# A hybrid decoder step on one core: earlier memory statistics, half-waits in the first quarters, and a head's output scaled on ScalarE

## What is computed

```python
hp = rms_norm(yp, g_norm[l])
qd, kd, vd, gd, qw, kw, vw, gw, qm, gm = split_projection(hp, w_in[l])
od = diff_attn_prompt(qd, kd, vd, lam, slopes_diff)      # 4 heads, softmax(q1 k1) - lam * softmax(q2 k2)
ow = dilated_prompt(qw, kw, vw, slopes_dil)
mk, mv = memory_kv(mem_prompt, g_mem_norm[l], w_mem_kv[l])   # rms_norm(mem) @ w_mem_kv
om = memory_attn(qm, mk, mv)
...
od = rms_norm(od, g_sub) * (1.0 - lam_init)              # per head, over its 256 values
cat = concatenate([od * silu(gd), ow * silu(gw), om * silu(gm)])
yp = yp + cat @ w_out
```

## Time and profile before

| | |
|---|---|
| median of 3 runs | 1027.82 us (1025.97 to 1028.28) |
| the profiled execution's own time | 1026.25 us |
| its span in the trace | 1024.5 us |
| granted TensorE clock | 0.997 |
| busy: PE, DVE, ACT, POOL | 1000.5, 723.7, 441.5, 54.7 us |

### The profile page before, as it was taken

The page is one execution under the profiler, slowest core; times in us unless marked ns, Lnnn a source line. Parts: engine busy times, 40 slices in busy tenths (PEclk is TensorE's granted clock), DMA queues, the critical chain, the costliest instruction groups (busy, mean ns, idle before and its releaser), DMA issues.

```text
span 1024.5 us, 24055 instructions
## 1 busy us (share of the span) xinstructions
PE 1000.5 (98%) x8103; PEld 980.4 (96%) x8103; DVE 723.7 (71%) x2687; ACT 441.5 (43%) x1169; POOL 54.7 (5%) x122
## 2 busy tenths in 40 slices
PE   7999999999999999999999999999999999999995
PEld 6899999999999999999999999999999999999995
DVE  5783267777788867778777676577774786588874
ACT  5763222222333333444342553335565365545552
POOL 0200000000000000000000000000000100000002
PEclk9999999999999999999999999999999999999998
DMA  9863288987978877777866686999662425234424
GB/s 300 250 195 107 64 266 265 293 271 226 266 220 254 259 231 235 219 224 207 245 200 192 186 249 181 231 280 284 193 191 72 140 74 153 94 104 145 124 84 167
DMA packets 254521, 203.33 MB, mean 198 GB/s; under 512 B 12480, under 2 KB 207670, under 8 KB 253750
## 3 DMA queue, kind: packets, MB, share of 16 engines
q1 hardware_dynamic: 253934, 200.67, 65.7%
q10 hardware_dynamic: 464, 1.12, 0.3%
HBM read 189.98 MB, written 11.76 MB: 197 GB/s over the span
## 4 chain that ended last, share of the span: by engine, by line
PE 91%; DVE 2%; ACT 2%; issue 2%; SPq 1%; DMA 1%; POOL 0%; DVEq 0%; POOLq 0%; ACTq 0%
PE z L1097 71%; PE z L1123 8%; PE o_ps L1193 2%; PE s_ps L1156 2%; PE t_ps L1143 2%; PE t_ps L1183 1%; PE s_ps L1161 1%; DMA w_raw<-in_w_mem_kv_dram 1%; PE o_ps L1198 1%; PE o_ps L1202 1%; PE s_ps L1168 1%; PE o_ps L1242 1%; ACT w_hi L1351 1%; PE s_ps L1028 1%; SPq L828 1%
## 5 line engine op out<-in xcount | busy, mean ns | idle before, releaser
L1097 PE MATMUL z<-act_hi,w_hi 128*128 128x260 f32 (+1 forms) x2048 | 440.9, 291 | 2.4 <-DVE act_lo L1629 2.3
L1097 PE MATMUL z<-act_hi,w_lo 128*128 128x260 f32 (+1 forms) x2048 | 422.4, 283 | 0.0
L1097 PE MATMUL z<-act_lo,w_hi 128*128 128x260 f32 (+1 forms) x2048 | 421.6, 282 | 0.0
L1097 PEld LDWEIGHTS z<-act_hi,w_hi 128*128 128x128 f32 x2048 | 321.5, 189 | 7.9 <-issue 4.0
L1097 PEld LDWEIGHTS z<-act_lo,w_hi 128*128 128x128 f32 x2048 | 319.9, 188 | 0.0
L1097 PEld LDWEIGHTS z<-act_hi,w_lo 128*128 128x128 f32 x2048 | 319.5, 188 | 0.0
L1676 DVE TENSOR_TENSOR w_lo<-w_raw,w_hi 128x512 fp32r<-128x512 f32 x302 | 206.8, 687 | 132.5 <-ACT w_hi L1351 131.8
L1351 ACT ACTIVATE w_hi<-w_raw 128x512 fp32r<-128x512 f32 x302 | 186.4, 626 | 200.4 <-PE z L1097 173.2
L1865 DVE CUSTOM_DVE_ANT_0 pages<-pages,q_bc 128x128 f32<-128x128 f32 x640 | 144.2, 285 | 21.2 <-DMA pages<-in_cache_k_win_dram 13.5
L1894 DVE SCALAR_TENSOR_TENSOR v_acc<-pages,dec_a,v_acc 128x256 f32<-128x256 f32 x224 | 94.3, 478 | 1.7 <-DMA pages<-in_cache_v_diff_dram 1.5
L1473 ACT ACTIVATE probs<-probs,st_n 128x128 f32<-128x128 f32 (+3 forms) x48 | 26.8, 558 | 79.9 <-DVE st_n L1804 79.6
(11 more groups left out here) (236 smaller groups left out, 1121.8 us busy)
## 6 DMA issues: line engine op xcount, KB each, us to landing
w_raw<-in_w_in_dram SPq DMA_DIRECT2D x224, 256.0 KB, 4.5
pages<-in_cache_k_diff_dram SPq DMA_DIRECT2D x128, 256.0 KB, 4.7
pages<-in_cache_v_diff_dram SPq DMA_DIRECT2D x128, 256.0 KB, 3.6
w_raw<-in_w_out_dram SPq DMA_DIRECT2D x64, 256.0 KB, 2.8
w_raw<-in_w_mem_kv_dram SPq DMA_DIRECT2D x32, 256.0 KB, 6.1
cat<-in_x_prompt_dram SPq DMA_DIRECT2D x8, 1024.0 KB, 6.0
q_bc<-q_rows_dram SPq DMA_DIRECT2D x32, 256.0 KB, 6.7
pages<-in_cache_mem_k_dram SPq DMA_DIRECT2D x16, 256.0 KB, 6.4
```

Source lines behind the costliest of these rows:

```text
L1097: last = nc.tensor.matmul(zb[:, bank, 0:b - a], lhs[:, w], rhs[:, kt, a:b], start=(kt == 0 and m == 0), stop=(kt == KT - 1 and m == 2))
```

## The change

There are four kinds of edits. In the tables of `plan()`, the memory squares go from slot 5 to 2 and the factor from slot 9 to 7; the first two key tiles are evacuated at slots 8 and 9 instead of 10 and 11, and turned at slots 10 and 11 instead of 11 and 13. `qrows` 2 goes from slot 177 to 178, and part 1 of the memory group's softmax from slot 196 to 195. In `quarter`, the first input tile and the first memory tile wait for the split activations before each pair of blocks instead of before all four. In a differential head, ACT waits for POOL's factor right behind the squares and scales `o_ps` into `o_nat` itself; DVE's scaling is dropped.

```diff
-    put(5, "mem", "squares")
-    put(9, "mem", "rstd")
+    put(2, "mem", "squares")
+    put(7, "mem", "rstd")
...
-            put(s + (6, 3)[n] if n < 2 else s, "evac", n, 0.65 if kind in ("gd", "gw") else 1.3 if kind == "gm" else 0.0)
+            put(s + (4, 1)[n] if n < 2 else s, "evac", n, 0.65 if kind in ("gd", "gw") else 1.3 if kind == "gm" else 0.0)
         if kind in ("mk", "mv", "kd", "kw", "vd", "vw"):
-            put(s + (7, 5)[n] if n < 2 else s + (2 if n < FIRST_IN else 1), "nat", n)
+            put(s + (6, 3)[n] if n < 2 else s + (2 if n < FIRST_IN else 1), "nat", n)
...
-    put(DONE[AT["qm", 3, 0]] + 1, "qrows", 2)
+    put(DONE[AT["qm", 3, 0]] + 2, "qrows", 2)
...
-                put(s0 + SOFT_AT[k], "soft", (what, k), 0.6)
+                put(s0 + SOFT_AT[k] - (what == MEMORY and k == 1), "soft", (what, k), 0.6)
...
                 if n == FIRST_IN:
-                    pe.wait_ge(s_plo, prep_base(2) + 2 * r + 2)
                     pe.wait_ge(s_xsl, 1)
-                if n == 0:
-                    pe.wait_ge(s_plo, 2 * r + 2)
...
                 for j in range(4):
                     kt = 4 * r + j
                     w = slice(j * P, (j + 1) * P)
+                    if n in (0, FIRST_IN) and j % 2 == 0:
+                        pe.wait_ge(s_plo, prep_base(0 if n == 0 else 2) + kt // 2 + 1)
...
                         nc.scalar.activation(o_nat[:, :], o_ps[:, 0:2 * P], ACT.Square,
                                              accum_out=st_q[:, 0, 0:1]).then_inc(s_osq, 1)
+                        act.wait_ge(s_orstd, what + 1)
+                        nc.scalar.activation(o_nat[:, :], o_ps[:, 0:2 * P], ACT.Copy, scale=st_q[:, 1, 0:1]).then_inc(s_ofree, 1)
...
                 if kind == "diff":
-                    dve.wait_ge(s_orstd, t + 1)
-                    nc.vector.tensor_scalar(o_nat[:, :], o_ps[:, 0:2 * P], st_q[:, 1, 0:1], None, ALU.mult).then_inc(s_ofree, 1)
+                    return
```

## The result

The changed kernel takes 1028.19 us (median of 22 runs, 1026.5 to 1030.95), the kernel before 1026.74 us (median of 22, 1025.82 to 1028.28). The ratio is 1.0015 with a 95% interval of 1.0009 to 1.0021: some 1.5 us slower, less than the 0.2% that the prediction called no change. Predicted was 1028.5 us. The profiled execution took 1027.94 us with a span of 1026.2 us. One execution each of three later kernels (*rows_early*, *soft_half*, *scale_only*) took 1407 to 5631 us; the ratios leave these three out, the medians still count them.

A forecast was written before the change was run, and what follows sets the result against it. PE was taken as the bound, busy 1000.5 of 1024.5 us, so only its waits counted. Key tiles +1.2, query rows +0.3 and memory softmax -0.8 gave +0.7 us on 1027.82, hence 1028.5 us, range 1025.0 to 1031.0.

The forecast's parts named there:

- likeliest case: Whole kernel: gains and losses balance as summed, or no move reaches PE's end; 1026.8 to 1029.8 us, chance 0.60.
- query rows: Slot 178: an old 0.8 us wait goes, a new 1.1 us wait comes near 567 us; net 0.3 us lost.
- key tiles: Start: ACT's second key copy waits for the first's store, ahead of split and squares; quarter 16 starts 1.2 us later.
- Half-waits, squares, factor: Start: half-waits gain at most 2.3 us, PE stands 2.3 us for diagonals; 0.6 us loss, hidden by the key tiles.
- Rival (a): Key and row stores land by themselves, key store in 1.9 us, both new waits vanish; -2.7 us, 1025.1, chance 0.18.
- Rival (b): Slot 178: the row store stays as slow as before, 3.8 us; +2.9 us, 1030.7, chance 0.18.
- The scaling: Sixteen differential heads: ACT gains about 0.8 us of wait and 0.3 us of scaling each, hidden; no cost taken.
- Rival (c): Differential heads: ACT, blocked about 1.1 us sixteen times, delays PE 0.3 us per step; +4.8 us, 1033.3, chance 0.04.
- Memory softmax: Part 1 one slot earlier no longer stands behind the bank's copy it waited for; 0.8 us gained.

The follow-up runs named there:

- rows_early: The changed kernel with the query rows' copy (`qrows` 2) back at slot 177; 1026.84 us, ratio 0.9997 to the kernel before.
- soft_half: The kernel before with only squares at slot 2, the half-waits and the softmax part one slot earlier; 1026.13 us, ratio 0.9987.
- scale_only: The kernel before with the scaling of the differential heads' output on ACT as its only edit; 1027.31 us, ratio 1.0001.
- factor_late: The changed kernel with the factor back at slot 9 and the first two key tiles' evacuation and turning where they were; 1027.37 us, ratio 1.0006.
- diag_first: rows_early with DVE building the factor's diagonals ahead of the split of quarter 10; 1026.25 us, ratio 0.9997 to the kernel before.
- head_only: The kernel before with only the edits of the start (squares, factor, first key tiles, half-waits); 1027.86 us, ratio 1.0008.
- dve_scale: The changed kernel with the scaling back on DVE; 1027.88 us, ratio 1.0002 to the kernel before.
- nat_late: diag_first with the second key tile turned at slot 13 again; 1024.35 us, ratio 0.9978 to the kernel before.
- rest_only: The kernel before with query rows at slot 178, softmax part at 195 and scaling on ACT, start unedited; 1028.92 us, ratio 1.0020.
- soft_only: The kernel before with part 1 of the memory softmax at slot 195 as its only edit; 1026.01 us, ratio 0.9992.
- after_again: The changed kernel timed once more, in the first batch of follow-ups; 1029.72 us, ratio 1.0029 to the kernel before.
- rows_late: soft_only with the query rows at slot 178, the scaling staying on DVE; 1026.18 us, ratio 0.9992 to the kernel before.

## Why the prediction was right, and where its terms were off

The time lies 0.3 us from the forecast, inside the likeliest case's own range, and part of that is luck. The median before that it was added to, 1027.82 us of 3 runs, was 1.1 us over the 1026.74 of 22, and the difference was 1.5 us where 0.7 were foretold; the two errors cancel in the sum. The term of the query rows was too small, that of the key tiles probably too large. (Two additions come out 0.1 us high: 28.1 + 0.35 + 3 x 1.42 is 32.7, and 566.5 + 0.80 + 0.91 is 568.2. Nothing hangs on them.)

**Half-waits, squares, factor: right in mechanism.** The wait for the diagonals was put at 2.3 us and was 1.1 to 2.0 us in five profiles; *factor_late* shows that the slot makes it, and *diag_first* that nothing is won by taking it away alone. Not foreseen was the wait for the weights of quarter 7: ACT's split, which waited for them, began at 24.20, and with DVE's PE could begin at 25.67. The step assumed that PE "ends near 25.8" with quarter 7; it began it then. And the prediction had this loss hidden by the next step, "which sets the time". In the changed kernel's own profile it was not: PE had no wait between the diagonals and the sample sums, and the half clock in that stretch took 1.7 us more for the same matmuls.

**Key tiles: the chain is real, but it did not hold in every execution, and its size was somewhat too large.** Foretold were a second copy at 39.65 by the end of the store, no more wait of 1.6 us, quarter 16 at 43.9, 1.2 us late, and PE waiting for `w_lo` at about 40 and 42.5. Seen in the changed kernel were 39.20 (38.51 to 39.00 in the five other profiles with this order) and no wait of 1.6 us, but the waits for `w_lo` were missing: its 1.7 us of delay came to it from the diagonals and the half clock. The 0.3 us for quarter 16's weights are in *head_only*, *dve_scale* and *diag_first*, at 42.76 to 43.25 us. So the 1.7 us near the foretold 1.2 are no proof of the step. The chain itself is shown by *nat_late*, at 1.9 us; over the executions the whole start costs 0.8 us (*head_only*, -0.1 to 1.7). That the landing doesn't hang on the issue shows as well: the first store was issued at 33.90 in *nat_late*, 34.61 in *diag_first* and 36.63 in the changed kernel, and let the second copy start at 39.94, 39.00 and 39.20. Rival (a), by which it lands on its own in 1.9 us, falls here. The Trainium skill's page, "DMA: Bandwidth & Descriptors", section "Anatomy of one DMA", would make it about 2.3 us from issue for 128 KB, as an estimate by its formula. The formula is for transfers that GpSimd issues, which the prediction did not say; SP issues these, and the three took 6.0, 4.3 and 2.5 us, and the measurement decides.

**Query rows: the step that was mis-sized.** It foretold a store in 1.6 us (1.4 measured), the first page at 564.7 and a wait of 1.1 us, net 0.3 us lost. Measured by runs, rows at slot 178 together with the scaling cost 2.9 us (*rest_only* against *soft_only*) or 1.8 us (the changed kernel against *rows_early*; 3.3 with *after_again*), each by ratios taken on different chips; the profile has 1.94 us of wait where 0.8 us were gained, net 1.1. The transfers were judged right: the squares of this head started at 555.75, 1.40 us behind the 554.35 of the prediction, and the pages came at 566.09, which is 564.69 on the prediction's scale. The step went wrong at its end, "the probabilities stand at 568.3, PE asks for them at 567.2". PE does not only need the probabilities but the bank, and ACT's sums, 1.23 us (569.40 to 570.63), hold it. With them the wait is 1.1 + 1.2 = 2.3 us and the term 1.5 instead of 0.3. The trace of the kernel before had it. The first and the last of the same eight instructions on its ACT:

```profile
566.24 0.26 ACT L1464 ACTIVATE t_ps<-t_ps 128x128 f32<-128x128 f32 x1
...
567.28 0.18 ACT L1464 ACTIVATION_READ_ACCUMULATOR t_ps<-t_ps 128x1 f32 x1
```

They end at 567.46, only 0.5 us before PE turns the probabilities; these, not the normalizing, were the last thing in front of it. Rival (b), a store of 3.8 us, did not happen; yet a good part of the wait of 3.3 us that it foretold, 1.9 to 2.5 us, came for this other reason.

**The scaling.** The prediction put 1.7 us of the rows' delay on it. The rows' copy stood 1.79 us behind the squares' start in the changed kernel and 0.37 in *rows_late*, 1.42 us of difference. Taken as an edit of its own it costs nothing, as foretold (*scale_only*, 1.0001). The trace of the changed kernel, instructions of line 1559:

```profile
L1559 ACT ACTIVATE o_nat<-o_ps,st_q x16: 474/476/478, 259.2 to 557.2; 128x256 f32<-128x256 f32 x16
its engine sat idle before it (us, times) until:
  POOL st_q L2228: 16.0, 16
```

Each is 476 ns, not the 0.3 us that was taken, behind 1.0 us of idle ACT, not 0.8; and no one waited for any. Rival (c), which priced this at 4.8 us, falls. Yet the two edits are not independent: the scaling is free where ACT has nothing urgent behind it, and in the one head where a copy for a store stood behind it, it decided between nothing (*rows_late*) and 2 to 3 us (*rest_only*).

**Memory softmax: right.** 0.8 us foretold, 0.8 measured (*soft_only*, interval 0.1 slower to 1.6 faster).

**What was left out entirely** is the granted clock. Corrected for the bank the sum would have been 1.2 + 1.5 - 0.8 = 1.9 us. Measured are 1.5 us on one chip and 3.0 (1.8 to 4.0) on the other, 0.8 + 2.9 - 0.8 = 2.9 us from the parts. The mean clock that each execution was granted says something of what the half clock does to the total. The profile of the kernel before, with 1.00 in every window read here, has a mean of 0.997, that of the changed kernel, with its stretch from 26.8 to 33.6 us, 0.994. Of the changed kernel's 22 executions six have 0.997, with a median of 1028.19 us, the same as that of all 22; nine have 0.994 or less, with 1028.89. The kernel before has medians of 1026.43 to 1026.87 us in its executions at 0.997, on the three chips. So the changed kernel's loss is there in full, 1.3 to 1.8 us, where the clock did not fall, near the corrected sum of 1.9; in executions with a low mean clock some 0.7 us are added. Nor does it make the wider spread (1027.2 to 1032.16 us in *after_again*, 1025.48 to 1026.69 in *soft_only*): the execution of 1032.16 us had 0.996. In *rest_only*, which has the start of the kernel before, none of 11 executions had 0.997, and in its profile the turnings and scores behind the stand took 3.3 us (568.83 to 572.11) instead of the 1.7 us of the changed kernel (570.77 to 572.46), where the clock stayed up. These 1.6 us could be what its loss of 2.9 us has over the term's 1.5. All this compares groups of executions and single profiles; no run takes the fall of the clock away and keeps the stand. What made *after_again* 1.5 us slower than the first comparison is open.

## What to carry to other kernels

When you work out whether a late result makes an engine wait, follow the bank or buffer that the waiting instruction needs, not the data alone: here the data were there 1.3 us before the bank. An instruction that waits for another engine is free or dear by what is queued behind it; look through every place where the pattern occurs for the one where a copy for a store follows. And behind an instruction that waits for a transfer whose landing the queue decides, put as little as possible: moving one turning by two slots was worth 1.9 us, more than the 1.5 us that the whole change cost in its first comparison.

## What the runs showed of the hardware that was not expected

PE's clock fell to half behind short stands, and not always. Single stands were followed by a granted clock of 0.50 at these lengths: 1.32 us (*factor_late*, at 25 us), 1.45 (*rows_early*), 1.71 (*diag_first*), 1.81 (*nat_late*), 1.84 (*after_again*, the diagonals), 1.85 (*soft_half*), 1.95 (*dve_scale*, at 570 us), 1.96 (*rest_only*) and 2.50 (*factor_late*, at 569 us). It stayed at 1.00 behind 1.94 (the changed kernel, at 570 us), 1.98 (*dve_scale*, the diagonals) and 2.04 us (*after_again*, at 569 us), and in *head_only* behind 1.28 and 1.41 us with one quarter between them. So the length of the stand does not decide it. Behind the stands of 1.96 and 2.50 us the clock was low as soon as PE came back; in the others PE first ran up to about 1.5 us at full speed. The Trainium skill, "TensorE: Matmul & The Clock Gate", Part 1, gives the clock two levels, 1.2 and 2.4 GHz; the traces agree, with windows at 0.50 and 1.00 and values between them where it changed inside a window. Three quarters took 5.97 instead of 4.27 us at the lower level. Whether the total pays for that hangs on what comes behind: *rows_early* and *nat_late* had such a stretch and were level with the kernel before and 2.3 us faster.

A store of 16 KB took 1.4 us to land where the DMA engines had moved 13 GB/s and less from 557.2 us on (it was issued at 557.82), and 3.8 us in the kernel before. The Trainium skill, "DMA: Bandwidth & Descriptors", section "Anatomy of one DMA", has a fixed cost of about 2.0 us, for the GpSimd path, and the 1.4 us of this one, issued by SP, lie under it.
